# The S5 layer's first input unit by row blocks, and four smaller moves around it

## The reference

```
h = rms_norm(x); q,k,v,u = h @ w_in            # first block: 8-head attention, causal conv (31 taps)
x = x + concat(attn, conv) @ w_out
x = x + (silu(h @ w_gate) * (h @ w_up)) @ w_down
# second block, layer 0: gated forgetting attention (16 heads), then swiglu; x += rmsnorm(result)
# second block, layer 1 (S5):
u  = rmsnorm(x) @ w_in                         # 1024 x 1024
y  = state-space scan of u, per group of 16 features, + d_skip * u
y  = gelu(y); y = y * sigmoid(y @ w_glu)
x += rmsnorm(y @ w_out); x += rmsnorm(swiglu(rmsnorm(x)))
```

## Time and profile before

| | |
|---|---|
| median of 3 runs | 980.24 us |
| the profiled execution | 980.41 us, of it span 978.5 us |
| PE busy | 961.0 us (98%), 5454 matmuls |
| PE weight loads | 803.0 us (82%) |
| DVE, ACT, POOL busy | 581.8, 507.0, 309.9 us |
| mean granted TensorE clock | 0.999 |

### The profile page before, as it was taken

The page is one execution under the profiler, slowest core; times in us unless marked ns, Lnnn a source line. Parts: engine busy times, 40 slices in busy tenths (PEclk is TensorE's granted clock), DMA queues, the critical chain, the costliest instruction groups (busy, mean ns, idle before and its releaser), DMA issues.

```text
span 978.5 us, 14303 instructions
## 1 busy us (share of the span) xinstructions
PE 961.0 (98%) x5454; PEld 803.0 (82%) x5454; DVE 581.8 (59%) x637; ACT 507.0 (52%) x727; POOL 309.9 (32%) x333
## 2 busy tenths in 40 slices
PE   8999999999999999999999999999989999999997
PEld 6988878888888888788888888888979888888886
DVE  4899775544554565665764554446686765445444
ACT  5866475444443467445664444435466664444432
POOL 5680458998687326761020000000000010000000
PEclk9999999999999999999999999999999999999999
DMA  9742036666877656545355666558936366557541
GB/s 332 259 157 86 1 117 214 220 222 218 283 225 236 202 195 212 174 130 172 108 193 175 192 192 229 199 174 275 383 140 216 129 189 198 172 178 251 173 171 43
DMA packets 133827, 186.79 MB, mean 191 GB/s; under 512 B 5904, under 2 KB 104720, under 8 KB 133264
## 3 DMA queue, kind: packets, MB, share of 16 engines
q1 hardware_dynamic: 109632, 158.28, 49.7%
q10 hardware_dynamic: 24144, 27.81, 8.2%
HBM read 174.54 MB, written 15.73 MB: 194 GB/s over the span
## 4 chain that ended last, share of the span: by engine, by line
PE 94%; DVE 3%; ACT 2%; issue 1%; POOL 0%; DVEq 0%; POOLq 0%; ACTq 0%
PE ps L519 25%; PE ps L490 17%; PE ps L492 16%; PE ps L491 16%; PE ps L470 2%; PE ps L1064 2%; PE ps L472 2%; PE ps L471 2%; PE ps L848 1%; PE ps L1641 1%; PE ps L1083 1%; PE ps L1074 1%; PE ps L630 1%; PE ps L1169 1%; PE ps L1020 1%
## 5 line engine op out<-in xcount | busy, mean ns | idle before, releaser
L422 DVE TENSOR_TENSOR wlo<-wraw,whi 128x2048 fp32r<-128x2048 f32 x127 | 301.7, 2377 | 291.6 <-ACT whi L416 291.6
L416 ACT ACTIVATE whi<-wraw 128x2048 fp32r<-128x2048 f32 x127 | 243.3, 1916 | 256.9 <-PE ps L492 160.5
L490 PE MATMUL ps<-whi,actH 128*128 128x512 f32 x640 | 257.9, 403 | 1.0 <-ACT qa L2130 0.6
L492 PE MATMUL ps<-whi,actL 128*128 128x512 f32 x640 | 250.2, 391 | 0.0
L491 PE MATMUL ps<-wlo,actH 128*128 128x512 f32 x640 | 249.4, 390 | 0.0
L490 PEld LDWEIGHTS ps<-whi,actH 128*128 128x128 f32 x640 | 120.3, 188 | 27.5 <-issue 2.1
L492 PEld LDWEIGHTS ps<-whi,actL 128*128 128x128 f32 x640 | 120.1, 188 | 26.2
L765 POOL TENSOR_SCALAR ss<-ss 128x1 f32<-128x1 f32 x8 | 1.8, 220 | 436.1 <-ACT sg L735 436.1
L491 PEld LDWEIGHTS ps<-wlo,actH 128*128 128x128 f32 x640 | 120.5, 188 | 22.3
L519 PE MATMUL ps<-whi,gH 128*128 128x512 f32 x248 | 77.8, 393 | 0.0
L519 PE MATMUL ps<-wlo,gH 128*128 128x512 f32 x248 | 76.8, 390 | 0.0
(11 more groups left out here) (454 smaller groups left out, 1573.4 us busy)
## 6 DMA issues: line engine op xcount, KB each, us to landing
wraw<-in_ffn_w_gate SPq DMA_DIRECT2D x44, 512.0 KB, 4.0
wraw<-in_ffn_w_up SPq DMA_DIRECT2D x44, 512.0 KB, 4.9
wraw<-in_ffn_w_down SPq DMA_DIRECT2D x18, 1024.0 KB, 4.9
wraw<-in_fox_w_in SPq DMA_DIRECT2D x16, 1024.0 KB, 5.6
wraw<-in_w_gate SPq DMA_DIRECT2D x22, 512.0 KB, 4.0
wraw<-in_w_up SPq DMA_DIRECT2D x22, 512.0 KB, 5.0
wraw<-in_w_in SPq DMA_DIRECT2D x9, 1024.0 KB, 11.3
wraw<-in_w_down SPq DMA_DIRECT2D x9, 1024.0 KB, 5.1
```

What stands on the lines that cost most here:

```text
L416: act.activation(self.high_of(n0), self.wraw[:, n0 % RAW, :], ACT.Copy).then_inc(self.hi_done, 1)
L422: dve.tensor_tensor(self.low_of(n0), self.wraw[:, n0 % RAW, :], self.high_of(n0).bitcast(F32), ALU.subtract).then_inc(self.lo_done, 1)
L490: pe.matmul(out, xh, wh, start=(ka == 0), stop=False)
L492: last = pe.matmul(out, xl, wh, start=False, stop=(ka == KT - 1))
```

## The change

1. `early_low` loses the entry of `f2`'s last down unit, so that its low part is written over its raw buffer, and the raw buffer (shared with unit `s`+3) is held until PE has used it. The entry of unit `s`+0 stays.
2. `s` is turned by row blocks with the helpers that `f2` uses (`pe_row_turn`, `act_row_turn`, `dve_row_turn`). The fillers and `pe_turn_plain` are gone. In the post-norm `pf0` the order on DVE and ACT is changed.
3. Unit `s`+0 is multiplied by a new `mm_tokens`: activations stationary, 256 weight columns moving, first row block 0, then row block 1. Its result has tokens on partitions; ACT copies it out, and PE transposes it back between the two halves of unit `s`+1.
4. Unit `s`+3 writes its second half into bank 0, and DVE starts on the first half when that is done.
5. `turn_inputs(0)` transposes all of `Vc`, then all of `Vs`.
6. `glu`: the gelu table is loaded before the last state swap; the third copy of the outputs, then gelu and high part of tiles 0 and 1, stand ahead of the last output copy; PE multiplies tile 0 ahead of the second `turn_outputs`; unit `glu`+0 uses banks 0 and 2.
7. Two of the four query copies are ahead of the table load.
8. Two semaphores of the conv norm share one counter.

```diff
-        self.early_low = {f["s"]: early["b"], f["f2.down"] + FT // 2 - 1: early["act"]}
+        self.early_low = {f["s"]: early["b"]}
...
+    def mm_tokens(self, pe, st, n0, r, bank):
+        pe.wait_ge(self.lo_done, n0 + 1)
+        out = self.ps[:, bank, r * 256:(r + 1) * 256]
+        for k in range(KT):
+            pe.wait_ge(*self.past(st + "_act_ready", KT * r + k + 1))
+            wh, wl = (t[:, k * 256:(k + 1) * 256] for t in (self.high_of(n0), self.low_of(n0)))
+            xh, xl = self.actH[:, k, r * P:(r + 1) * P], self.actL[:, k, r * P:(r + 1) * P]
+            pe.matmul(out, xh, wh, start=(k == 0), stop=False)
+            pe.matmul(out, xh, wl, start=False, stop=False)
+            last = pe.matmul(out, xl, wh, start=False, stop=(k == KT - 1))
+        if r == RT - 1:
+            last.then_inc(self.used, 1)
...
     # dve_postnorm
-        dve.wait_ge(*self.past(st + "_squares", 3))
+        dve.wait_ge(*(self.past(first[:2] + "_second", 1) if st == "pf0" else self.past(st + "_squares", 3)))
         norm(2)
         if turn:
             turn(0, range(4))
         dve.wait_ge(*self.past(st + "_squares", 4))
         norm(3)
         if turn:
-            turn(0, range(4, KT))
+            turn(0, (4, 5) if st == "pf0" else range(4, KT))
...
         for c in range(2):
             add(1, c)
+            if st == "pf0" and c == 0:
+                turn(0, (6, 7))
...
     # PE
-            s_first, s_rest, late = m.pe_turn_plain(pe, "s", "pf0_x_ready", (4, 5, 6, 7, 2, 3), 40)
-            m.pe_ffn(pe, "f2", f2_turn, last_units=2, half=lambda: s_first(0), end=lambda: s_first(1))
-            s_rest()
-            for i in range(4):
+            s_turn = lambda r, part: m.pe_row_turn(pe, "s", "pf0_x_ready", ROWS_HIGH, r, part)
+            m.pe_ffn(pe, "f2", f2_turn, last_units=2, half=lambda: s_turn(0, 0), end=lambda: s_turn(0, 1))
+            m.mm_tokens(pe, "s", first["s"], 0, 0)
+            s_turn(1, 0)
+            s_turn(1, 1)
+            m.mm_tokens(pe, "s", first["s"], 1, 0)
+            for i in range(1, 4):
+                if i == 3:
+                    pe.wait_ge(*m.past("ut1", 1))
+                m.mm_features(pe, first["s"] + i, i, middle=tokens_turned if i == 1 else None,
+                              second=0 if i == 3 else None)
...
-                pe.wait_ge(*m.past("vc_a", 3 + b if b > 0 else 3))
-                for q in range(4 * b, 4 * b + 4):
-                    cols = slice((q % 4) * P, (q % 4 + 1) * P)
-                    last = pe.transpose(ps[:, b, cols], m.Vc[:, q, :], idn[:])
-                    if b == 0:
-                        last = pe.transpose(ps[:, 4, cols], m.Vs[:, q, :], idn[:])
+                parts = ((m.Vc, b, 3 + b),) if b > 0 else ((m.Vc, 0, 1), (m.Vs, 4, 3))
+                for src, bank, ready in parts:
+                    pe.wait_ge(*m.past("vc_a", ready))
+                    for q in range(4 * b, 4 * b + 4):
+                        last = pe.transpose(ps[:, bank, (q % 4) * P:(q % 4 + 1) * P], src[:, q, :], idn[:])
...
-            turn_outputs(1)
...
             for i, k in enumerate(Y_ORDER):
+                if i == 1:
+                    turn_outputs(1)
                 pe.wait_ge(*m.past("yg_act_ready", i + 1))
...
     # ACT, query heads
+            m.act_heads(act, "a1", m.qt, (0, 4), (4, 5), 0)
             act.activation(rinv[:, 0, 0:1], m.halfpi[:], ACT.Exp)
-            m.act_heads(act, "a1", m.qt, (0, H1), (4, 5), 0)
+            m.act_heads(act, "a1", m.qt, (4, H1), (4, 5), 2)
...
     # ACT, S5
+            act.wait_ge(m.used, n + 1)
+            act.activation(m.sg[:], ps[:, 0, :], ACT.Copy).then_inc(sem("s_tokens"), 1)
...
+            act.activation(m.nmax[:, 0, 0:1], m.halfpi[:], ACT.Gelu_apprx_tanh)
             states_swapped(3)
-            act.activation(m.nmax[:, 0, 0:1], m.halfpi[:], ACT.Gelu_apprx_tanh)
             outputs_out(2)
...
+            for i in range(2):
+                yg_gelu(i)
+                yg_high(i)
+            outputs_out(3)
```

More of the change, by code:

```diff
@@ L107, in resolve @@
             counts["ao"] = counts["fo"] = KT // 2
-            for s in ("f1", "fp", "f2", "f3"):
+            for s in ("f1", "fp", "f2", "s", "f3"):
                 counts[s] = RT * KT
@@ L455, in low_piece, with mm_features @@
                           ALU.subtract).then_inc(done, 1)
-    def mm_features(self, pe, n0, bank, it=0, ready=None, order=range(KT), middle=None, late=None):
-        pe.wait_ge(self.lo_done, n0 + 4 * it + 1)
+    def mm_features(self, pe, n0, bank, order=range(KT), middle=None, second=None):
+        pe.wait_ge(self.lo_done, n0 + 1)
         high, low = self.high_of(n0), self.low_of(n0)
@@ L462, in mm_features @@
             out = self.ps[:, bank, f * TOK:(f + 1) * TOK]
+            if second is not None and f == 1:
+                last.then_inc(self.sem("features_half"), 1)
+                out = self.ps[:, second, 0:TOK]
             for i, k in enumerate(order):
[L464 to L467, removed]
                 c = k * 256 + f * P
@@ L649, in dve_row_turn @@
                .then_inc(self.sem(st + "_act_ready"), 1)
[L651 to L681, removed]
     def pe_spread(self, pe, st, bank):
@@ L730, in act_post_square @@
             act.wait_ge(*self.past(st + "_scale", 1))
-        act.wait_ge(*(self.past(first, 1), self.past(st + "_normed", 1), self.past(first[:2] + "_second", 1),
-                      (self.used, used))[i])
+        second = self.past("pf0_normed", 3) if st == "pf0" else self.past(first[:2] + "_second", 1)
+        act.wait_ge(*(self.past(first, 1), self.past(st + "_normed", 1), second, (self.used, used))[i])
         if i > 1:
@@ L1668, in second_sums @@
                                      start=True, stop=True)
-                last.then_inc(sem("ln_second"), 1)
+                last.then_inc(sem("ln_total"), 1)
             def spread_norm():
@@ L1832, in _, with tokens_turned @@
                            lambda: f2_turn(0, 0), lambda: f2_turn(0, 1))
-            s_first, s_rest, late = m.pe_turn_plain(pe, "s", "pf0_x_ready", (4, 5, 6, 7, 2, 3), 40)
-            m.pe_ffn(pe, "f2", f2_turn, last_units=2, half=lambda: s_first(0), end=lambda: s_first(1))
-            s_rest()
-            for i in range(4):
-                m.mm_features(pe, first["s"] + i, i, ready="s_act_ready" if i == 0 else None,
-                              late=late if i == 0 else None)
+            s_turn = lambda r, part: m.pe_row_turn(pe, "s", "pf0_x_ready", ROWS_HIGH, r, part)
[4 more added lines that the diff above has]
+            m.mm_tokens(pe, "s", first["s"], 1, 0)
+            def tokens_turned():
+                pe.wait_ge(*m.past("s_tokens", 1))
+                for f in range(2):
+                    for r in range(RT):
+                        c = f * TOK + r * P
+                        last = pe.transpose(ps[:, 0, c:c + P], m.sg[:, r * 256 + f * P:r * 256 + (f + 1) * P], idn[:])
+                last.then_inc(sem("s_features"), 1)
+            for i in range(1, 4):
[3 more added lines that the diff above has]
+                              second=0 if i == 3 else None)
                 if i == 1:
@@ L2300, in _, with yg_gelu, yg_high @@
             outputs_out(1)
+            act.activation(m.nmax[:, 0, 0:1], m.halfpi[:], ACT.Gelu_apprx_tanh)
             states_swapped(3)
-            act.activation(m.nmax[:, 0, 0:1], m.halfpi[:], ACT.Gelu_apprx_tanh)
             outputs_out(2)
[L2304 to L2313, removed]
+            def yg_gelu(i):
+                yg = m.ygT[:, Y_ORDER[i], :]
+                act.wait_ge(*m.past("y_sum", i + 1))
+                act.activation(yg, yg, ACT.Gelu_apprx_tanh).then_inc(sem("gelu"), 1)
+            def yg_high(i):
+                kt = Y_ORDER[i]
+                act.wait_ge(*m.past("gelu", i + 1))
+                act.activation(m.actH[:, kt, :], m.ygT[:, kt, :], ACT.Copy).then_inc(sem("yg_high_ready"), 1)
+            for i in range(2):
+                yg_gelu(i)
+                yg_high(i)
+            outputs_out(3)
+            for i in range(2, KT):
+                yg_gelu(i)
+                if i > 2:
+                    yg_high(i - 1)
+            yg_high(KT - 1)
             n = first["glu"]
@@ L2653, in _ @@
             n = first["s"]
[L2654 to L2655 removed]
+            m.dve_postnorm(dve, "pf0", 0, m.gb[1], "gain1_in", 16, "f2_first",
+                           lambda r, kts: m.dve_row_turn(dve, "s", ROWS_HIGH, r, kts, MIXPRE + 8))
             m.dve_scale(dve, "s")
```

46 lines of the change are left out of this document (26 added, 20 removed), and 2 rows, old and new, of the table KINDS.

## The result

The changed kernel takes 985.94 us (median of 6 runs, 984.87 to 986.75); the kernel before, in the same session, 980.12 (6 runs, 979.33 to 980.32). The ratio is 1.0062, 95% interval 1.005 to 1.0074: 5.8 us slower. The forecast was 977.7, so 8.2 us are missing.

The account below looks back on a forecast made before the run. PE's own work, 94% of the span, was taken as the bound. Gains 1.30 + 1.05 + 0.10 + 0.44 - 0.30 = 2.6, and 0.17 for the median, off 980.41 gave 977.65, say 977.7 us; range 976.5 to 978.9.

Parts of the forecast that it names:

- Query copies: Third head fill of the query heads: PE's wait behind the table load goes whole, gain 1.30 us.
- Turn into S5: From f2's end into S5: turning by row blocks gains 1.5, four transposes back cost 0.43; net gain 1.05 us.
- C: Rival: turning by row blocks into S5 gives 0.3 instead of 1.05, the gate loses 0.5; 978.6 us, chance 14%.
- Held buffer and late loads: SP's loads behind f2's held raw buffer land 5.0 us after issue, at 688, wanted at 698: cost nothing.
- Two banks: S5's last unit: PE's first wait goes, but the next transposes still need ACT's Ur copy; gain 0.10 us.
- B: Rival: two-bank edit gives 0.8, gate edit nothing or a little, 3.6 in all; 976.7 us, chance 10%.
- Turned inputs: Ahead of the scan: four of eight transposes run in a gap, so the whole scan moves up; gain 0.44 us.
- Gate product: Step from scan into gate product: gelu and high parts ahead make the last output copy late; loss 0.30 us.
- Rival D: Clock falls at gaps of the turn into S5, 684 to 688.4, losing 5.8; about 983.5 us, 6% with other losses.
- a low clock after 683: Listed sign that the prediction is wrong: a low granted TensorE clock after 683 us in the execution; no size given.

Follow-up runs that it names:

- experiment 7: The changed kernel with both 4 MB table loads issued by SP behind the weight loads, instead of by ACT: 976.77 us, ratio 0.9971.
- the first run of experiment 9: The changed kernel with both first glu loads ahead of s+3 on SP, and ACT's two Ur copies ahead of glu+1's high part: 976.87 us.
- experiment 1: The kernel before with one line of the change: f2's last down unit loses its early_low entry, so its raw buffer is held: 987.96 us.
- experiment 2: The changed kernel with the first two glu loads issued ahead of s+3 on SP: 977.10 us, ratio 0.9973.

## Why the prediction was wrong

- **Query copies, 1.30: right.** The third head fill follows the second by 1.83 us without a wait; the scores behind are 1.94 earlier, 0.65 of it there from the start. Alone: 1.5.
- **Turn into S5, 1.05: right.** From the end of `f2`'s slot (680.58) to unit `s`+1 (689.50) it is 8.92 us against 10.33, forecast 8.7. PE's waits are 0.35, 0.21 and 0.50. The four transposes back make unit `s`+1 0.43 longer (6.19 against 5.76), with no wait. Net 0.98. C falls.
- **Held buffer and late loads, nothing: this is the step that failed.** The text was: "Such a load lands 5.0 us after issue, so at 688; ACT wants it only after unit 1, at 698 ... These cost nothing." The order on SP was seen and the buffer's release (682.7, in fact 680.8) too. But only the first of the three loads took 5.1; the two behind took 22.9 and 32.5. The row was taken from loads that had the engines nearly to themselves (issued up to 672), and the row of the `glu` loads in the same view is already slower (7.3, shown above). It was then used for a stretch in which two tables of 4 MB run. In the kernel before, those tables, issued at 683.59 and 693.11, took 12.9 and 15.9 us, so one or both were under way from 683.6 to 709.0, and the `glu` units, issued at 674.72 and 676.92, had landed by 681.4 and 684.8. "Wanted at 698" was said of `s`+3 (in fact 696.6). The `glu` units were wanted at about 702.1 and 707.9 (by experiment 7, where PE and not a load holds their high parts). So the first was 1.9 us late and the second 6.4. With a landing of 27 us in the sum, the loss would have been on the page. What it measured: 6.3 us of wait of PE and 2.0 to 2.7 of low clock.
- **Two banks, 0.10: right in kind.** It gave nothing (0.70 of wait became 0.73), 0.1 less than forecast. The reason, ACT's high part ahead of the `Ur` copy, is shown by the first run of experiment 9. B falls with it.
- **Turned inputs, 0.44: right**, 0.44 by the trace.
- **Gate product, -0.30: right in kind**, -0.2 by the trace, -0.4 by the runs.
- **Rival D, 983.5,** was nearest to the measured time, for a wrong reason. It put the low clock at the turn and its price at 5.8. The clock fell over 25 us later, behind a wait for weights, and cost less than half of that; experiment 1 shows it without the turn. The forecast's own sign of being wrong, a low clock after 683, did come, but as a consequence of the wait.

The sum without the failed step is what experiment 2 measured: 2.6 forecast, 2.6 measured. Taken from the traces the terms are 1.29 + 0.98 - 0.03 + 0.44 - 0.2 = 2.5. Two executions can differ by more than such a term (0.65 us above), so an agreement to a tenth is in part luck. Still open is why the first `glu` unit took 22.9 us in one run and 27.5 to 30.1 in three others, while the second, issued 0.6 us behind it in the same queue, always took 32.2 to 32.5.

## What to carry to other kernels

When an edit changes which event frees a buffer, list everything that stands behind that load in the issuing queue, and move all of it in time. Price each transfer by the stretch that it moves into, with what other queues carry there, and not by its landing in a calm one. Where an in-order engine consumes a late transfer, look for the small instruction behind it that another engine needs: reordering the loads (experiment 2), or putting the big transfers behind the urgent ones in the same queue (experiment 7), removed the whole cost here without giving up the edit.

## What the runs showed of the hardware

- A load of 1 MB with small packets took 5.0 us with the engines nearly to itself and 20.9 beside two tables in another queue, whose packets were 20.6 KB on average. Two such loads took 20.7 on average beside one table. Beside both tables the two took 27.7 to 31.3 on average. With the tables in their own queue, behind them, they took 9.3 on average.
- From 692 to 701 two queues moved 250 and 251 packets; the bytes were 0.24 and 3.54 MB.
- A wait of 6 to 7 us brought the granted clock from 1.00 to 0.50 for the 5 us from 715 to 720 and part of the next 2, at a price of 2.0 to 2.7 us in this stretch. Gaps of up to 0.5 us, with PE busy 2.36 of 3 us, left it at 1.00.
